# RWKV-7 rounds: B, K and V turned by unit-matrix products with one copy a set, and fillers mixed into a level's first products

## The reference, cut to what matters

```
def step(S, inp):                       # _rwkv7_scan, one token
    rt, wt, kt, vt, kkt, at = inp
    sa = einsum('rbhvk,rbhk->rbhv', S, -kkt)
    S = S * wt[..., None, :] + sa[..., None] * (kkt * at)[..., None, :] + vt[..., None] * kt[..., None, :]
    return S, einsum('rbhvk,rbhk->rbhv', S, rt)
```

## Time and profile before

| | |
|---|---|
| median of three runs | 2029.03 us |
| the profiled execution: its own time, its span | 2030.1 us, 2028.3 us |
| PE busy, share of the span | 1836.2 us, 91% |
| ACT busy | 606.9 us, 30% |
| DVE busy | 961.1 us, 47% |
| first to last `lt`/`tz`/filler product (L2001) | 683.7 to 1042.9 us |
| one round in the middle, 830.59 to 869.89 | 39.3 us |

### The profile page before, as it was taken

One profiled execution on the slowest core, in us unless ns is written; L12 is line 12 of the kernel. 1 busy time (PEld: TensorE's weight loads), 2 busy tenths in 40 slices (PEclk: granted clock), 3 DMA queues, 4 the chain that ended last, 5 costly groups with the idle time before them and its releaser, 6 DMA issues. The chain is left out here.

```text
span 2028.3 us, 49121 instructions
## 1 busy us (share of the span) xinstructions
PE 1836.2 (91%) x20798; PEld 1727.9 (85%) x20798; DVE 961.1 (47%) x1619; ACT 606.9 (30%) x1339; POOL 780.0 (38%) x622
## 2 busy tenths in 40 slices
PE   6499799998899678888876999999999999999998
PEld 3488799787899577777755999999999999999998
DVE  7701854578433545555537455242424242424264
ACT  4412244333113555655533232020101010101034
POOL 3502242343762323235535313434343434344460
PEclk8699899899999799999997999999999999999999
DMA  9555110102111000000013101111111111111112
GB/s 310 176 186 195 29 38 21 30 1 97 41 40 29 6 7 6 4 4 5 5 37 109 38 22 36 48 37 47 36 47 36 47 38 49 37 52 31 52 53 94
DMA packets 148182, 110.33 MB, mean 54 GB/s; under 512 B 13298, under 2 KB 144393, under 8 KB 147757
## 3 DMA queue, kind: packets, MB, share of 16 engines
q1 hardware_dynamic: 148013, 107.83, 17.4%
HBM read 93.17 MB, written 14.55 MB: 53 GB/s over the span
## 5 line engine op out<-in xcount | busy, mean ns | idle before, releaser
L253 PE MATMUL banks<-Z_r 128*128 128x384 f32 x2016 | 350.8, 334 | 0.0
L253 PEld LDWEIGHTS banks<-Z_r 128*128 128x128 f32 x2016 | 349.5, 188 | 0.2
L2733 DVE SCALAR_TENSOR_TENSOR XT<-banks,MOD,XT 128x128 f32 x224 | 110.8, 516 | 226.0 <-PE banks L253 225.2
L3067 ACT ACTIVATE PAD<-banks 128x384 f32<-128x384 f32 x96 | 47.2, 492 | 503.0 <-PE banks L2962 502.7
L235 POOL TENSOR_TENSOR Z_r<-Z,ones 128x512 fp32r<-128x512 f32 x56 | 77.1, 1376 | 254.4 <-DMA Z<-in_mlp_w 254.4
L235 POOL TENSOR_TENSOR W_r<-Z,ones 128x1024 fp32r<-128x1024 f32 x32 | 77.1, 2409 | 240.7 <-DMA Z<-in_mlp_w 240.7
L3183 DVE TENSOR_TENSOR PAD<-PAD 128x384 f32<-128x384 f32 x96 | 99.1, 1032 | 142.7 <-ACT PAD L3067 142.6
L2962 PE MATMUL banks<-HT_r,W_r 128*128 128x384 f32 x768 | 149.1, 335 | 2.5 <-ACT HT_r L3034 1.6
L2962 PE MATMUL banks<-YT_r,W_r 128*128 128x384 f32 x768 | 148.6, 334 | 0.0
L2962 PE MATMUL banks<-HT_r,Z_r 128*128 128x384 f32 x768 | 148.5, 334 | 0.0
L2962 PEld LDWEIGHTS banks<-HT_r,W_r 128*128 128x128 f32 x768 | 134.4, 188 | 3.4 <-issue 1.9
(11 more groups left out here) (415 smaller groups left out, 3952.5 us busy)
## 6 DMA issues: line engine op xcount, KB each, us to landing
Z<-in_w_mod SPq DMA_DIRECT2D x16, 1024.0 KB, 5.2
Z<-in_mlp_w SPq DMA_DIRECT2D x32, 512.0 KB, 4.2
Z<-in_mlp_w SPq DMA_DIRECT2D x58, 256.0 KB, 2.7
YT<-in_w_in SPq DMA_DIRECT2D x18, 512.0 KB, 3.9
XT<-in_w_mod SPq DMA_DIRECT2D x8, 1024.0 KB, 10.8
residual<-Z SPq DMA_DIRECT2D x1, 4608.0 KB, 17.5
low_part<-XT_r SPq DMA_DIRECT2D x1, 4608.0 KB, 15.4
XT<-low_part SPq DMA_DIRECT2D x8, 576.0 KB, 5.5
```

The costliest lines, as they stand in the source:

```text
L253: mm = nc.tensor.matmul(self.bank(slot, g), w[slot][:, k, :], x(k, g), start=(n == 0 and k == 0), stop=(n == 2 and k == self.blocks - 1))
L2733: ins = nc.vector.scalar_tensor_tensor(out=x, in0=S.PS[3 * slot + g][:, a:b], scalar=S.MOD[:, ds(col, 1), c:c + 1].rearrange("p a b -> p ( ...
L3067: nc.scalar.activation(R[slot][:, grp(g)], up.bank(slot, g), ACT.Relu).then_inc(up.drained[g].sem, 1)
```

## The change: what it does

Three edits, all in the rounds' preparation:

1. The odd fillers no longer transpose 128x128 blocks. For each chunk c, pair p and half h they multiply the 64x64 block by the unit matrix (`near(1, left, unit, "turned")`), so that the turned block lands on the partitions of its own half, already in the layout of `Bt`, `Kt` and `Vt`: twelve products in place of three transposes.
2. `turned_act` then needs one copy of 128x384 in place of four of 64x192.
3. The filler behind `lt_run(d, i)` is now issued in turn with it, product by product (where the filler has six products, two of `lt_run` for each of its own). The filler 3i-1 moves from between the two `tz_pe` to behind the second.

```diff
@@ filler
-            for p in range(NP):
-                src = {"B": C.BT[par][:, d, p, :], "K": C.KT[:, d, p, :], "V": S.Z[:, 6 + p, tok:tok + P]}[x]
-                if x == "K" and p == 0:
-                    done(pe, "k_rows", n, d + 1)
-                run.append(((lambda p=p, src=src: nc.tensor.transpose(S.PS[1][:, p * P:(p + 1) * P], src, S.ident[:, :])), None))
-            run[-1] = (run[-1][0], "turned")
+            if x == "K":
+                done(pe, "k_rows", n, d + 1)
+            left = {"B": tokens(C.BT[par], d), "K": tokens(C.KT, d),
+                    "V": lambda c, p, y, h: S.Z[y, 6 + p, tok + N * c:tok + N * c + N]}[x]
+            run = near(1, left, unit, "turned")
@@ round_pe
-                    alternate(lt_run(d, i))
-                    alternate(beside)
+                    far = lt_run(d, i)
+                    if len(beside) == len(far):
+                        alternate(far, beside)
+                    else:
+                        alternate(far[0::2], far[1::2], beside)
                 for d in range(2):
                     tz_pe(pe, n, d, i)
-                    if d == 0:
-                        beside = filler(pe, n, 1 - par, 3 * i - 1, a)
-                        alternate(beside)
+                alternate(filler(pe, n, 1 - par, 3 * i - 1, a))
@@ turned_act
-        for c in range(2):
-            for h in range(2):
-                src = S.PS[1][rows_of(c), 0:NP * P].rearrange("p (q h n) -> p q h n", h=2, n=N)[:, :, h, :]
-                ins = nc.scalar.copy(x[rows_of(h), d, c, :, :], src)
-        ins.then_inc(f["copied"].sem, 1)
+        nc.scalar.copy(x[:, d, :, :, :].rearrange("p c q n -> p (c q n)"), bank(1)).then_inc(f["copied"].sem, 1)
```

## The result

The changed kernel takes 2050.78 us (median of four runs, 2049.63 to 2052.35), the kernel before beside it 2028.77 (four runs, 2025.78 to 2032.57). The ratio is 1.0114 with the interval 1.0092 to 1.0135: 22 us slower, where 1999 us, 30 faster, was forecast. 2050.8 is also outside the range.

What follows compares the result with a forecast made beforehand. It took PE's half-used quarters and turned rows on PE and ACT to set the pace; gains of 3.74 us a round less 0.45 for supply gave 3.3, times nine rounds 30 us, so 1999 us (8 in 10: 1991 to 2019).

Steps and rivals of the forecast that it cites:

- the last term of the sum: PE's instruction supply: one more mid-run pause a round, 0.45 us set against the gains, bounds 0 and 1.8.
- The rest of the walk: Step-by-step pricing of one round, levels 1 to 4 and round's end: gains sum to 3.74 us a round.
- the one stop in the earlier trace: A PE run stopping in its middle for 0.92 us with no wait in the profile, about once a round.
- The reading of the bound: Rounds of 39.3 us: unmixed runs leave half of PE's quarters unused; turned rows stand in the way on PE and ACT.
- The pause of 0.25 us: Unexplained PE pause inside a run, between level 2's second products and level 3's first; kept in the forecast.
- Pairs at 0.75 us: `lt_run` in turn with a filler of twelve products: 48 records taking 0.75 us, bounds 0.71 and 1.68.
- Rivals A and B: Mixed pairs: A, half the overlap, 2022 us, chance 0.11; B, runs fully serial, 2046 us, chance 0.08.
- One copy at 0.48 us: ACT's single 128x384 copy of turned rows takes 0.48 us in place of 1.29 for four copies.
- Levels 1 to 4: Stretch from level 1's first product to the next round's first: 21.92 us before, forecast near 18.6.
- level 1: First products of level 1 to level 2's: 5.96 us now, gain 1.13, DVE then the last waited for.
- The end of the round: Last level's second products to next round's product: 2.76 us becomes 2.99, a loss of 0.23.
- Rival C: PE's instruction supply: two to three more 0.92 us pauses a round cut the gain to 1.4, 2016 us; chance 0.09.

Runs made afterwards that it cites:

- e2: Kernel before with only the unit-matrix products and the one copy, fillers in their old order: 2045.82 us, ratio 1.0102.
- e8: Kernel before with half the copies of turned sets 2 and 5 on DVE instead of ACT: 2026.09 us, ratio 0.9991.
- e7: Kernel before with only the Gram fillers (k = 0, 4, 6, 10) mixed into `lt_run`, no instruction more: 2020.79 us, ratio 0.9973.
- e10: Kernel before with Gram fillers mixed into `lt_run` and only the last filler 3i-1 moved behind direction 1's second products: 2031.49 us, ratio 1.0027.
- e9: Changed kernel with filler 3i-1 back between the two `tz_pe`; products, one copy and mixing kept: 2042.33 us, ratio 1.0101 to the kernel before.
- e13: Changed kernel with Gram products BT by RR merged with BT by AR, 96 PE instructions a round fewer: 2047.92 us, ratio 1.0081 to the kernel before.
- e12: Kernel before with Gram fillers mixed in, Gram products merged (96 instructions fewer) and 24 unread tiny products a round added: 2028.32 us, ratio 1.0012.
- e3: Kernel before with 63 unread 64x64x1 products a round added, 252 PE instructions: 2051.77 us, ratio 1.0118.

## Why the prediction was wrong

The step that failed is the last term of the sum: "I set one more pause of half that size, 0.45, against it (bounds 0 and 1.8)". Measured: 7.58 - 1.65 = 5.93 us of issue waits more a round, in 27 more stops over six rounds, which also grew from 0.51 us each to 1.05 (at packets' ends: 13 stops, then 40). The forecast missed the round by 41.66 - 36.0 = 5.66 us, so this term is nearly the whole error (5.93 - 0.45 = 5.48). The rest of the walk came true: busy time and waits for other engines fell by 3.58 us a round, where it said 3.74. The bound was wrong as well. It was made of the one stop in the earlier trace rows and the share of added records; it should have been made of the pace of the packets. The row that tells was there: the page's queue of instructions, 137 packets, and the strip above. At 3.26 us at the least, the 10.06 packets of a round of before can't take less than 32.8 us, and 11.05 not less than 36.0. The forecast lay exactly on that floor, with nothing to spare for packets at their usual distance. At the mean distances of e2 and of the changed kernel, 3.61 and 3.73 us, 11.05 packets make 39.9 and 41.2.

Point by point:

- **The reading of the bound.** I took what bounds PE to be the quarters of the array in use and its waits for ACT and DVE. With 3.93 us a packet the kernel before stood 5 to 8% from the pace at which the change and e2 run. So a gain much beyond that was not to be expected even without an added instruction; no run here tests how far it could go. The pause of 0.25 us "that nothing explains" is the end of a packet too.
- **Pairs at 0.75 us.** Right: `XT` from 867.48, the last `YT,misc` 868.19, 0.71 us for 48 records; also where the products of a turned filler take part. Rivals A and B are out. The Trainium skill's rule on row tiles and one PSUM bank ("TensorEngine Tiling (Array Packing)", "Gotcha 1: PSUM Pressure"), which would have made them serial, does not hold for this pattern. The prediction's argument was too short, since the 48 records go to two banks and not to one; but 24 of them went into one bank from both halves of the rows in 0.71 us, 30 ns each, and a record of 64 columns alone would fill its quarter for some 55 (an estimate: the records of 130 columns of L1414 in the kernel before start 0.11 us apart).
- **One copy at 0.48 us.** Right (a mean of 476 ns in six rounds). e8, which halves ACT's part of two of the six sets, found no gain from it by itself.
- **Levels 1 to 4.** 18.6 us were forecast, and 17.4 are left without the stops. So the walk's gains are there, but the supply takes them back and more. In level 1 it was to be DVE that PE waits for last; DVE's Gram mask ended at 864.72, and PE stood until 865.74 at the end of a packet. e7 takes those gains that need no instruction and gets 0.3%.
- **The end of the round.** Forecast 0.79 + 0.27 for the move, measured 1.2 a round in e10. In the changed kernel the way from the last level's second products to the next round is 3.14 us (880.97 to 884.11), with 2.99 forecast, and taking the move back (e9) gained nothing that is clear of the noise.
- **Rival C.** It named the mechanism and had 0.09. It was sized in the same way as the term, by stops of 0.92 us, "two to three" a round; 4.5 came. That is why even it ended at 2016. "Against: the densest stretches of today, 96 records in 1.64 us, show no pause" was a wrong inference: a stretch of 192 instructions fits into one packet. What decides is how fast 256 instructions in a row would go, against the 3.3 us or more until the next are there.

The Trainium skill ("Runtime: NRT & Kernel Launch", "Instruction fetch mechanics") says that an engine's instruction memory is refilled in blocks of 16 KiB, 256 instructions, and that crossing into the next block is mostly hidden. The trace agrees with the size (0.98 MB in 60 packets) and not with the hiding: 42.1 us of stops at the packets' ends in six rounds.

**What stays open.** Why a packet starts only 1.0 us or more behind PE's restart, and why PE needs another 1.1 to 1.6 us behind its end, is not shown. Nor is it settled how the cost grows with the number: e2 has 67 packets at 3.61 us, e13 has 64 at 3.88 and a round nearly as long as the change's; e7 and e12 have the same number of instructions, 0.4% apart. Where in a round a packet ends, and so which wait a stop falls on, may be the difference; no run here tells. And e3 was disturbed by the clock.

## What to carry to other kernels

Count PE's instructions, not only its time. In a stage of many small products, divide the stage's time by the packets of the instruction queue in it; when that comes near the least spacing found anywhere in the trace, an edit that adds instructions can cost by their number even if it makes every engine less busy, and one that merely packs them closer gains little (e7: 0.3%). A transpose of 128x128 that shows as one record and one load is then worth more than four quarter products that show as eight of each, though these save three of ACT's four copies.

Try the parts that add no instruction by themselves: here the one that could be kept (e7) was hidden in a change that lost. And put what the next stage waits for ahead of what only fills.

## What the runs showed that was not expected

- The packets of instructions never come nearer than 3.26 us in any kernel, and 256 PE instructions are in each; all 480 stops of PE inside the rounds fall on their ends. One fp32 product counts four of them (two matmul records, two loads), a transpose two.
- Products of one column are not free: 63 of them cost 1.29 us in the one round at full clock, and with them the granted clock fell to 0.92 in four of six rounds, where the kernel before has 1.00 throughout. What did that is open.
